# Value pages ordered behind the score groups, and first key stores behind the third group, in a two-layer decoder step

## What is computed

```python
def shared_kv(x, kv_norm_w, w_kv, k_norm_w):
    kv = rmsnorm(x, kv_norm_w) @ w_kv
    k, v = jnp.split(kv, 2, axis=-1)
    k = rmsnorm(k.reshape(B, T, MOBA_HEADS, MOBA_HD), k_norm_w)      # 8 heads of 128
    return k, v.reshape(B, T, MOBA_HEADS, MOBA_HD)                   # both are outputs

def per_seq(args):                       # moba_sample, for each of the 8 sequences
    q_s, kn, vn, pages = args
    k_past = cache_k[pages].reshape(past, MOBA_HEADS, MOBA_HD)       # 2 pages of 128 rows
    v_past = cache_v[pages].reshape(past, MOBA_HEADS, MOBA_HD)
    ...
    return moba_attend(q_s, q_pos, k_s, v_s, rel_bias)               # softmax(q k + bias) v
```

## Time and profile before

| | us |
|---|---|
| median of 3 runs | 501.35 (500.54 to 501.76) |
| profiled execution | 499.29 |
| its span | 497.4 |
| PE busy in the span | 489.1 |
| DVE busy | 359.0 |
| ACT busy | 260.7 |

### The profile page before, as it was taken

The page is one execution under the profiler, slowest core; times in us unless marked ns, Lnnn a source line. Parts: engine busy times, 40 slices in busy tenths (PEclk is TensorE's granted clock), DMA queues, the critical chain, the costliest instruction groups (busy, mean ns, idle before and its releaser), DMA issues.

```text
span 497.4 us, 9895 instructions
## 1 busy us (share of the span) xinstructions
PE 489.1 (98%) x3685; PEld 423.8 (85%) x3685; DVE 359.0 (72%) x633; ACT 260.7 (52%) x536; POOL 96.5 (19%) x139
## 2 busy tenths in 40 slices
PE   7999999999999999999999999999989999999997
PEld 6889978899788997799799999987757778999885
DVE  3865539894698829896389987998966764775662
ACT  6735533565417724375454364764737655556630
POOL 0291003720063200920000042446002000000000
PEclk9999999999999999999999999999999999999999
DMA  9993978999899998999956899989798477683211
GB/s 264 368 330 118 278 252 304 371 367 238 266 333 394 261 233 300 348 361 238 261 169 211 294 298 224 280 224 220 239 298 281 154 229 234 232 307 124 86 53 53
DMA packets 86770, 125.54 MB, mean 252 GB/s; under 512 B 5491, under 2 KB 51524, under 8 KB 86596
## 3 DMA queue, kind: packets, MB, share of 16 engines
q1 hardware_dynamic: 85874, 124.63, 80.6%
q0 software_dynamic: 768, 0.28, 0.4%
q10 hardware_dynamic: 82, 0.02, 0.0%
HBM read 98.93 MB, written 27.57 MB: 254 GB/s over the span
## 4 chain that ended last, share of the span: by engine, by line
PE 88%; DVE 3%; DMA 3%; ACT 2%; issue 1%; SPq 1%; DVEq 0%; ACTq 0%
PE bank L940 44%; PE bank L937 18%; PE bank L921 7%; PE bank L1049 3%; DMA w_raw<-in_ret_w_in 3%; PE bank L1169 2%; PE bank L1063 1%; PE bank L996 1%; PE bank L1111 1%; PE bank L1215 1%; ACT rows L1504 1%; DVE small L1737 1%; PE bank L1029 1%; PE bank L1030 1%; PE bank L1031 1%
## 5 line engine op out<-in xcount | busy, mean ns | idle before, releaser
L1579 DVE TENSOR_TENSOR w_lo<-w_raw,w_hi 128x512 fp32r<-128x512 f32 x207 | 145.1, 739 | 62.8 <-ACT w_hi L1239 62.0
L1239 ACT ACTIVATE w_hi<-w_raw 128x512 fp32r<-128x512 f32 x208 | 118.6, 620 | 65.8 <-PE bank L940 35.4
L940 PE MATMUL bank<-xn_hi,w_hi 128*128 128x320 f32 x320 | 100.2, 317 | 0.2 <-DVE raw_qk L1669 0.2
L940 PE MATMUL bank<-xn_hi,w_lo 128*128 128x320 f32 x320 | 97.6, 309 | 0.0
L940 PE MATMUL bank<-xn_lo,w_hi 128*128 128x320 f32 x320 | 97.5, 309 | 0.0
L937 PE MATMUL bank<-w_hi,xn_hi 128*128 128x512 f32 x160 | 64.8, 405 | 0.0
L940 PEld LDWEIGHTS bank<-xn_hi,w_hi 128*128 128x128 f32 x320 | 59.7, 188 | 4.2 <-issue 2.7
L937 PE MATMUL bank<-w_lo,xn_hi 128*128 128x512 f32 x160 | 62.5, 391 | 0.0
L937 PE MATMUL bank<-w_hi,xn_lo 128*128 128x512 f32 x160 | 62.4, 390 | 0.0
L940 PE MATMUL bank<-ym_hi,w_hi 128*128 128x320 f32 x192 | 60.9, 317 | 0.0
L940 PEld LDWEIGHTS bank<-xn_lo,w_hi 128*128 128x128 f32 x320 | 59.8, 188 | 0.2
(11 more groups left out here) (289 smaller groups left out, 780.1 us busy)
## 6 DMA issues: line engine op xcount, KB each, us to landing
w_raw<-in_ret_w_in SPq DMA_DIRECT2D x23, 1024.0 KB, 11.0
st<-in_state_ret SPq DMA_DIRECT2D x32, 512.0 KB, 8.2
out_ret_state_sample<-st SPq DMA_DIRECT2D x32, 512.0 KB, 4.6
w_raw<-in_ret_w_out SPq DMA_DIRECT2D x8, 1024.0 KB, 8.7
w_raw<-in_moba_w_in SPq DMA_DIRECT2D x8, 1024.0 KB, 6.5
w_raw<-in_w_kv SPq DMA_DIRECT2D x8, 1024.0 KB, 8.1
cache<-in_cache_v SPq DMA_DIRECT2D x16, 512.0 KB, 4.9
cache<-in_cache_k SPq DMA_DIRECT2D x44, 128.0 KB, 4.5
```

The costliest lines, as they stand in the source:

```text
L940: mm = pe.matmul(bank[out][:, 0:T], w[:, wk, P * tile:P * tile + P], x[:, k, :], **flags)
L1239: act.activation(w_hi[:, c % 2, part], w_raw[:, c % RAW, part], ACT.Copy).then_inc(w_hi_done, 1)
L1579: dve.tensor_tensor(w_lo[:, c % 2, part], w_raw[:, c % RAW, part], w_hi[:, c % 2, part].bitcast(F32), ALU.subtract).then_inc(w_lo_done, 1)
```

## The change

Value pages 16, 17 and 18 are no longer issued between the key pages. Pages 16 and 17 are issued right behind `tb`, which waits for KS 3; pages 18 and 19 at SN. The three stores of the first half of the new keys are issued at the step KS 2, behind a wait for the end of that group on TensorE. The stores of the second half stay at KX 2. No other engine's program is changed.

```diff
-ORDERED_AT = {8: 1, 9: 2, 10: 3, 11: 4, 12: 7, 13: 10, 14: 11, 15: 12, 16: 13, 17: 14, 18: 15}
+ORDERED_AT = {8: 1, 9: 2, 10: 3, 11: 4, 12: 7, 13: 10, 14: 11, 15: 12}
@@
                     sp.dma_start(tb[:, :, :], bass.AP(scratch.tensor, FAR - P, [[skew, P], [LINE, MH], [1, TP]]))\
                         .then_inc(tb_loaded, 16)
-                elif kind == "KX" and step[1] % 2 == 0:
-                    p = step[1] // 2
+                    load_page(16)
+                    load_page(17)
+                elif step in (("KS", 2), ("KX", 2)):
+                    p = int(kind == "KX")
+                    if p == 0:
+                        await_ks(sp, 2)
                     for n, t in enumerate(tile_order("mk", p, 1)):
                         m = TOK[t][1]
                         sp.wait_ge(rows_done, 3 * p + n + 1)
                         sp.dma_start(k_out[t][:, 512 * p:512 * p + 512], rows[0:m, t, :]).then_inc(rows_stored, 16)
                 elif kind == "SN":
-                    load_page(16 + NCP - 1)
+                    load_page(18)
+                    load_page(19)
```

## The result

The change makes the kernel slower: 503.73 us (502.09 to 506.83) against 501.35 (499.8 to 503.63), both medians of 11 executions. The ratio is 1.0057, with a 95% interval of 1.0039 to 1.0075. The forecast was 500.7, with a range of 499.0 to 503.1. The profiled execution took 503.08 us with a span of 501.0.

A forecast was written before the change was run, and what follows sets the result against it. TensorE, busy 98%, was taken to bound the kernel, tied with the key-row chain. KS 2's 2.18 us gap goes, but the stores' new wait lets only 0.6 us reach the end: 501.35 - 0.6 = 500.75, rounded to 500.7; range 499.0 to 503.1.

The forecast's parts named there:

- The frame: Whole kernel: the end moves by no more than the start of ScalarE's first key row copy of chunk 39.
- the first: KS 2: the gap stays, stores wait behind it; 1.6 us slower, 502.95 us; chance 0.16.
- the second: First-half key stores: gap goes, but stores land in 4.8 to 7.1 us; 503.15 to 505.5 us; chance 0.07.
- KS 2 loses 2.2 us for want of code: Third score group on TensorE: 4.87 us against 2.69 for KS 3, a 2.18 us loss from late code.
- The code packet of 362 meets an emptying queue. I take the 2.18 us of KS 2 as gone: KS 2: queue drained by 363.0 at the latest, so the gap goes; bounds 0 and 2.18 us.
- The rule of the Trainium skill: Code fetch at KS 2: block crossings are mostly hidden, so less traffic would not remove the 2.18 us.
- Store landings, taken as 2.4 us: Third first-half key store behind KS 2: lands 2.4 us after issue, range 2.0 to 2.8.
- SyncE's reaction and the spacing: SyncE behind KS 2: acts 0.24 us after its end; third store issued 1.12 us later.
- The moved value pages cost nothing: Pages behind KS 3: chunk 42 may hold ScalarE 1.6 us, but 9 us of cover makes the cost nothing.
- The tie in the kernel before: Around 367.99: the third store, landing at 367.65, and the ScalarE/VectorE chain are about level with TensorE.
- Rival 3: Stretch of the stores: the 2.1 us between profiled execution and median lies there and goes too; 498.7 us; chance 0.20.
- VectorE's wait for key page 15: VectorE until 365.02: the 2.08 us wait goes, worth nothing to the end.

The follow-up runs named there:

- e9: Kernel before with value pages moved as in the change, stores left at KX 0, chunk 40 issued right behind chunk 39: 498.47 us against 501.32, ratio 0.9943.
- e10: The change with weight chunk 40 issued right behind chunk 39: 501.48 us against 501.32, ratio 1.0.
- e11: Kernel before with weight chunk 40 issued right behind chunk 39, value pages and stores as before: 498.62 us in one run.
- e3: The change with only 16 of 128 partitions of weight chunk 40 loaded: 501.42 us in one run.
- e12: The change run again unaltered, for a second profile: 504.17 us in one run.
- e4: The change with weight chunk 41 issued behind KS 3, no longer right behind the three stores: 504.49 us in one run.
- e1: Kernel before with only the value pages moved as in the change, stores left at KX 0: 501.49 us against 501.4, ratio 0.9988.
- e7: Kernel before with value pages moved as in the change, stores at KX 0, and TensorE's code shifted by 120 instructions: ratio 0.9975.
- e8: Kernel before run again unaltered, for a second profile: 499.84 us in one run.
- e2: Kernel before with only the three stores moved behind KS 2, value pages left between the key pages: 504.76 us against 501.4, ratio 1.0066.
- e5: The change with TensorE's code shifted by 120 instructions: 500.93 us in one run.
- e6: Kernel before with TensorE's code shifted by 120 instructions: 503.0 us in one run.

## Why the prediction was wrong

The frame held: the end moved by what the key row copy of chunk 39 moved. The rival that came true is the first, with a part of the second on top.

- **That KS 2 loses 2.2 us for want of code:** right. The shifted code takes the gap away, and so does lighter traffic.
- **"The code packet of 362 meets an emptying queue. I take the 2.18 us of KS 2 as gone":** this is the step that failed. I had computed rightly that chunk 40 and page 15 drain by 363.0, and did not ask by when the packet had to start. It had to start near 360.5, inside the time of that traffic (in e9, e10, e11 and e3 it started 0.3 to 1.0 us ahead of KS 2, once that traffic was lighter). What the change removes stands behind it in the queue. The trace of before held the number: the packet's end at 363.7 against the resumption at 365.08 shows 1.4 us from the one to the other, so a packet that starts at 363.0, in an empty queue, is too late by 2.5 us. Size of the error: 5.15 - 2.69 = 2.46 us.
- **The rule of the Trainium skill** ("Runtime: NRT & Kernel Launch", "Instruction fetch mechanics"), that the fetch is mostly hidden, gave the right sign through the wrong reason: the gap is a fetch that isn't hidden. Its blocks of 256 instructions fit the runs. KS 2 has 128 weight loads and 128 matmuls and stalled in front of its last 16 instructions, so nearly a whole block is used up in the 2.3 us up to there; 120 instructions more ahead of it, and it no longer stalled.
- **Store landings, taken as 2.4 us:** mis-sized. They took 4.2 in the change, 4.0 and 4.1 in e12 and e4, 2.8 to 3.1 at best. I had taken stores of the y rows, each by itself, for three in a row. Error: 1.8 us, of which 0.4 to 0.7 are three stores in a row and the rest goes with the code packet that ran beside the third. Of the range of 2.0 to 2.8 for this term the later runs reach only the upper end (e3, e10) or lie above it.
- **SyncE's reaction and the spacing:** 0.13 and 1.17 us, for 0.24 and 1.12. Right.
- **The sum again with the measured terms:** 360.85 + 5.15 + 0.13 + 1.17 + 4.2 + 0.1 = 371.6. The forecast was 367.4; of the 4.2 us between them 2.46 are the gap and 1.8 the landing.
- **The moved value pages cost nothing:** right (e1, e10). They were said to be a neutral part, and e1 shows it: 0.9988.
- **The tie in the kernel before:** right, and it is why moving the pages alone brings nothing while KS 2 has its gap. The prediction let the third store land at 367.65; by the trace it is 360.64 + 7.28 = 367.92, 0.07 us ahead of ScalarE. In e7, e8, e9 and e11, where the store is earlier, the copy starts 2.15 us behind the end of KS 2, which would be 367.80 here, so the store held it by 0.2 us. e9 has both holds removed and gains 0.57%.
- **The size:** the median moved by 2.4 us and the ratio says 2.9, against 3.6 in the profiled pair. By the last column of the table the mean of two executions each gives 10.5 - 7.4 = 3.1.
- **Rival 3, that the 2.1 us between the profiled execution and the median lie in this stretch:** it did not come true, and about half of them have a source elsewhere, the clock (last section).
- **VectorE's wait for key page 15, said to be gone:** 1.09 us of the 2.08 are left. They cost nothing, as had been said.

The chances were too low where they should have been joined: a gap that stays (0.16) and a store that lands late (0.07) were priced as if only one could be, at 1.6 and 1.8 us, and the two together lie outside the range.

## What to carry to other kernels

When a stall is laid to a full transfer queue, work out by when the held-up transfer had to start, and look at what was issued ahead of that time: only that traffic counts for this stall, and moving what is issued later does nothing about it. A transfer that frees a buffer should not be put behind a wait for compute when its landing is near the path already: the wait's delay, its position in the queue and the whole landing time are added up in front of the next user. And price several transfers in a row by rows of several in a row.

## What the runs showed of the hardware

**Code in dense stretches.** 256 instructions in 2.7 us were too fast for the supply of code under traffic. The packet of 0.02 MB needed 0.96 to 1.4 us on its engine, and TensorE resumed 1.3 to 1.6 us behind its end. With the packet at 1.4 to 2.3 us behind the start of KS 2, seven profiles with the code in its old place had a gap of 1.6 to 2.2 us; with it 0.3 to 1.0 us ahead, four had none.

**The clock after a stand.** In the change TensorE stood for 1.9 us in KS 2, and its granted clock fell from its full to its half level (1.2 GHz) for 3.4 us:

```profile
366.00:367.00 1.00, 1.00 (x6) 0.83 (x3) 0.51 (x1) 0.00 (x0) 0.00 (x0) 0.50 0.00 0
367.00:368.00 1.00, 1.00 (x4) 0.78 (x3) 0.00 (x0) 0.00 (x0) 0.00 (x0) 0.50 0.65 133
368.00:369.00 1.00, 1.00 (x4) 0.81 (x3) 0.00 (x0) 0.00 (x0) 0.00 (x0) 0.50 0.95 334
369.00:370.00 1.00, 1.00 (x5) 0.78 (x5) 0.00 (x0) 0.00 (x0) 0.00 (x0) 0.79 0.99 219
```

The 8 projections behind KS 2 took 369.51 - 366.00 = 3.5 us and not 367.60 - 365.65 = 1.95 as before. In the change this is hidden, since ScalarE waits for the store until 371.61. In e1 it is not: a stand of 2.2 us, the clock at half level for 3.4 us, and the key rows start at 8.85 instead of the 7.57 of the kernel before run again. The kernel before run again stood as long (2.2 us) and kept its clock. So such a stand can cost its own length and about 1.5 us more, but does not always. It is the same at the key transposes: in e2, e4 and e5 TensorE waited 2.1 to 2.2 us for the rows there, the clock fell for 3.4 us, and from the transposes to the end it took 118.5 to 118.7 us; in e3, e6, e10 and e12, which waited as long and kept their clock, 117.1 to 117.3.

One such stretch is 0.003 of the mean granted clock, and the executions differ in how many they have. Of the 61 executions of the kernel before that ran beside the experiments, 34 had a mean clock of 0.999 or 1.000 and took 500.4 us on the mean; 22 had 0.995 to 0.997 and took 502.6; five had 0.993 and took 504.1. The execution that was profiled for the prediction had 1.000, so a sum that starts from it and is compared with a median of 501.35 contains about 1 us of clock. The change, too, took 502.9 us in its four executions at 1.000, 2.5 more than the 27 at 1.000 of the kernel before (500.5). That the clock makes these differences is read from their going together; no run sets it.
